# Attention values gathered by group of heads, a modulation slab moved ahead of a branch weight, and four filler matmuls taken out

## The chip, the cores and the metric

The kernel runs on one core of one Trainium2 chip. The metric is the device time of one execution in microseconds (us).

## The reference

Two transformer blocks are computed in sequence on 256 tokens of width 1024, in fp32. The part that the change touches lies in the first block's token mixer: eight attention heads of 64 values share two key and value heads, and the mixer's two branches are then merged.

```python
def blocked_bidirectional_gqa(q, k, v):
    ...
        s = jnp.einsum('bhgqd,bhkd->bhgqk', qblk, kt) * scale
        p = jax.nn.softmax(s, axis=-1)
        return jnp.einsum('bhgqk,bhkd->bhgqd', p, vt)
...
    ya = jnp.einsum('bsw,wd->bsd', o_att.astype(h.dtype), w_branch_att)
    yh = jnp.einsum('bsw,wd->bsd', o_hg.astype(h.dtype), w_branch_hg)
    g = jax.nn.sigmoid(gate_logits.astype(f32)).reshape(B, S, N_BRANCHES, D)
    merged = (g[:, :, 0] * ya.astype(f32) + g[:, :, 1] * yh.astype(f32)).astype(h.dtype)
    return jnp.einsum('bsd,de->bse', merged, w_out)
...
        x = x + gate1 * token_mixer(...)
        h = rms_norm(x, norm_ffn_w[l]) * (1.0 + scale2) + shift2
        x = x + gate2 * expert_choice_ffn(h, w_router[l], w_exp_gate[l], w_exp_up[l], w_exp_down[l])
```

`gate1`, `scale2` and so on are six vectors of 1024 values, products of the conditioning vector with `ada_w`. The mixer is followed by 16 experts (400 MB of weights) and by the second block.

## The kernel before, in words

Each engine has its own program, written out in order; semaphores tie them together. Three orders matter here.

**The weights.** SP loads slabs of 2 MB, in the order of `FIRST_SLABS`, into a ring of three slots (`slot_of`), then the experts' slabs. `slab_free` makes SP wait until the slot's slab before has been used. A slab of `ada_w` (`ada4`, `ada5`, ...) is read by TensorE as it lies. All others (`W9`, `W10`, `att`, `hg`, `out0`, ...) are first split by half slab, called a chunk: ScalarE writes a rounded part (line 784), VectorE the remainder (line 1287), and TensorE multiplies three times (lines 2069 to 2071). There are three chunk buffers. `att` is the weight of the attention branch; its halves are the chunks of the jobs `ya0` and `ya1`. `hg` and `yh0`, `yh1` are the same for the other branch.

**PSUM.** Work on TensorE is cut into jobs. The list `JOBS` gives each job one of four pairs of PSUM banks, and `begin` makes a job wait until the job before it on its pair is drained.

**The tail of the mixer on TensorE** is, in order: `a_values` for two halves of heads of token tile 0 (jobs `pv00`, `pv01`, line 2243), `W9`, the same for tile 1 (`pv10`, `pv11`), `ada9`, a transpose, `ada4`, the small column job `adc9`, the first half of `W10`, the row job `adr4`, the second half of `W10`, `ada5`, `ya0`, `adr5`, `ya1`, `yh0`, `yh1`. An `ada` job (line 2156) multiplies a slab by the conditioning vector; VectorE copies the result out (`ada_part`, line 1339); the row job (line 2177) sums it and repeats it over all partitions, and VectorE adds it to the bias (`ada_row`, line 1356). `adr4` and `adr5` make the two halves of `gate1`, which is first read after `mo0`.

In `a_values`, `b` picks two of the four heads of a group and their output goes to PSUM partitions 64b to 64b+63, 256 columns wide. `attended` (line 1523) copies it to `oattT`, whose four blocks of 128 rows so follow the natural order of the 512 rows of `w_branch_att`.

Earlier, `level(0)` issues four matmuls on constant data (`spin_into`, line 2080), whose result is overwritten, before it waits for its inputs (`factors_ready` and the draining of `W0`).

Of the kernel before, what the change touches and what calls it, by code (L numbers as in the profile page):

```python
# [14 lines left out]
P = 128  # L15
S = 256
T = S // P
D = 1024
# [43 lines left out]

# [15 lines left out]
FIRST_SLABS = (  # L78
    [(f"ada{i}", f"ada{i}") for i in range(4)]
    + [(n, n) for n in ("W1", "W2", "W0", "W4", "W5", "W3", "W6", "W7", "ada6", "W8", "ada7")]  # L80
    + [(n, n) for n in ("W9", "ada8", "ada9", "W10", "ada4")] + [("att", "ya1"), ("ada5", "ada5"), ("hg", "yh1")]
    + [("out0", "mo0"), ("ada10", "ada10"), ("ada11", "ada11"), ("out1", "mo1")]
)
A_SLABS = [("v0", "v0"), ("v1", "v1"), ("u0", "u0"), ("u1", "u1"), ("am0", "am0"), ("am1", "am1")]
# [102 lines left out]
ARRIVED, BEFORE, _count, _last = [], [], [0] * (R + 4), [None] * (R + 4)  # L187
for _n in range(AT_FFN[1] + 2 * FJ):
    _s = slot_of(_n)
    _count[_s] += 16  # L190
    ARRIVED.append(_count[_s])
    BEFORE.append(_last[_s])
    _last[_s] = _n
# [11 lines left out]
def build(nc, A, out):  # L205
    with ExitStack() as ctx:
# [339 lines left out]
        def _(sp):  # L546
# [34 lines left out]
            for name, _ in FIRST_SLABS:  # L581
                n = SLAB_AT[name]
                if name.startswith("ada"):
                    load(n, columns(A["ada_w"][0], int(name[3:]) * NB))
                elif name == "W5":
                    load(n, columns(A["w_in"][0], W_COLS[name], 256), dst=kn(n)[:, :, 0:256])
                elif name.startswith("W"):
                    load(n, columns(A["w_in"][0], W_COLS[name]))
                elif name in ("att", "hg"):
                    load(n, A[f"w_branch_{name}"][0].rearrange("(k p) n -> p k n", p=P), 4)  # L590
                else:
                    load(n, columns(A["w_out"][0], int(name[3:]) * NB))

# [676 lines left out]
        def _(dve):  # L1270
# [247 lines left out]

            def attended(job, t, g):
                wait_full(dve, job)  # L1520
                dst = oattT.rearrange("p (i s) -> p i s", i=4)[:, 2 * g:2 * g + 2, t * P:(t + 1) * P]
                src = bank(job, 0)[:, 0:S].rearrange("p (i s) -> p i s", i=2)
                dve.tensor_copy(dst, src).then_inc(psum_drained[pair(job)], 1)

            maxima(0, "sc00")
# [44 lines left out]
            ada_part(4)  # L1570
            ada_col(9)
            split_to(CHUNK_OF["ya0"])
            dve.wait_ge(bias1_in, 32)
            ada_row(4, gate1[:, 0:NB])
            split_to(CHUNK_OF["ya1"])
            ada_part(5)
            split_to(CHUNK_OF["yh0"])

            for job in ("W7", "W8"):
# [1 line left out]
            for n in range(2):  # L1581
                job = f"ya{n}"
                wait_full(dve, job)
                for t in range(T):
                    dve.tensor_tensor(merged[:, t, n * NB:(n + 1) * NB], bank(job, t),
                                      gsig[:, 0, t, n * NB:(n + 1) * NB], ALU.mult).then_inc(psum_drained[pair(job)], 1)

                if n == 0:
                    ada_row(5, gate1[:, NB:D])
                split_to(CHUNK_OF["yh1"] + n)  # L1590
            for job in ("W9", "W10"):
                wait_drained(dve, job)
# [443 lines left out]
        def _(pe):  # L2036
# [163 lines left out]
            def level(lv):  # L2200

                job = f"lv{lv}"
                begin(job)
                if lv == 0:
                    spin_into(4, bank(job, 1)[:, 0:S])
                if lv:
                    pe.wait_ge(exp_ready, 4 * lv - 2)
                pe.wait_ge(factors_ready, lv + 1)
                queries = EQ[lv % 2] if lv else gq
                if lv == 0:  # L2210
                    wait_drained(pe, "W0")
                for t in range(T):
                    for h in range(HG):
                        qry = t if lv < LEVELS - 1 else 1 - t
                        ins = mm(bank(job, t)[:, h * P:(h + 1) * P], EK[lv % 2][:, h, t * P:(t + 1) * P],
                                 queries[:, h, qry * P:(qry + 1) * P], start=True, stop=True)
                end(ins, job)
# [17 lines left out]
            def a_values(t, g):  # L2235
# [2 lines left out]
                wait_drained(pe, f"PT{t}{g}")  # L2238
                begin(job)
                for k in range(2):  # L2240
                    heads = ptr[g][:, k * NB:(k + 1) * NB].rearrange("p (j b s) -> p b j s", j=2, b=2)
                    for b in range(2):
                        ins = mm(PS[64 * b:64 * b + 64, 2 * pair(job), 0:S], va[:, k, 64 * g:64 * g + 64], heads[:, b],
                                 start=k == 0, stop=k == 1)
                end(ins, job)

            def gated_values():
# [52 lines left out]
            turn("ohgT", [ohg[:, t, i * P:(i + 1) * P] for i in range(4) for t in range(T)])  # L2300
            ada_part(4)
            ada_col(9)
            natural("W10", hT, lambda: ada_row(4))
            ada_part(5)
            pe.wait_ge(oatt_low, 1)
            branch("ya0", oattR)
            ada_row(5)
            branch("ya1", oattR)
            wait_drained(pe, "ohgT")
            for n in range(2):  # L2310
                branch(f"yh{n}", ohgR)
# [443 lines left out]
```

## Time and profile before

| | |
|---|---|
| median of 3 runs | 1819.2 us (1819.18 to 1823.26) |
| the profiled execution: its own time | 1823.26 us |
| the profiled execution: span from first to last instruction | 1821.4 us |
| mean granted TensorE clock | 0.888 |
| busy: TensorE, VectorE, ScalarE, GpSimd | 81%, 32%, 26%, 5% of the span |
| busy in the chain that ended last | DMA 45%, TensorE 42%, VectorE 6% |

The profile has a page with shares of the span, and views that can be asked of any stretch: the instructions in order of time (a timeline), busy time by stretch, and the chain of work that ended last. In a timeline a row is start, duration, engine, line, operation, what is written and read, count of merged instructions, and in brackets the idle time before it with what ended it. One fp32 matmul appears as two records. In a row by stretch, the columns are: stretch, its length, then busy time (and instructions) of TensorE, its weight loads, VectorE, ScalarE and GpSimd, then the granted clock as a share of 2.4 GHz, the busy share of the DMA engines, and GB/s. The mixer fills the first 285 us or so, the experts follow until about 1200 us, then the second block.

### The profile page before, as it was taken

The page shows a single profiled execution, that of the slowest core. Times are in us where ns is not written, and L with a number is a line of the kernel's source. Part 1 is how long each engine was busy: PE and PEld are TensorE (multiplying, and loading weights), DVE is VectorE, ACT ScalarE, POOL GpSimd, SP SyncE. Part 2 cuts the span into 40 slices and gives each one's busy share as a digit, 9 for nine tenths or more (in the row PEclk, how much of TensorE's full clock was granted, in tenths as well). Part 3 has the DMA queues.
Part 4 walks back from the last instruction along what each step waited for, and adds up shares of the span by engine and source line. Part 5 has one row for each costly group of instructions (what it writes and reads, how often), then busy time and mean ns, then how long its engine had stood idle before and what let it go on. Part 6 is the DMA issues. An engine that isn't in the chain of part 4 may idle for free.

```text
span 1821.4 us, 21033 instructions
## 1 busy us (share of the span) xinstructions
PE 1471.9 (81%) x8909; PEld 932.2 (51%) x8909; DVE 582.5 (32%) x749; ACT 467.0 (26%) x660; POOL 89.5 (5%) x77
## 2 busy tenths in 40 slices
PE   4999998777666776677667667679999989979998
PEld 1987674222221222123212222138799978869997
DVE  3488463000000000000000000037665555755553
ACT  3676322000000000000000000035554445664442
POOL 1591000000000000000000000000000000000000
PEclk8999998977888877887778877879999999999999
DMA  9536789999999999999999999994455535425540
GB/s 353 172 123 224 269 331 368 427 429 428 429 429 429 427 430 427 429 429 426 431 427 429 429 427 431 425 365 170 175 194 187 187 140 200 147 93 185 185 185 24
DMA packets 97860, 565.30 MB, mean 310 GB/s; under 512 B 4764, under 2 KB 6056, under 8 KB 73224
## 3 DMA queue, kind: packets, MB, share of 16 engines
q1 hardware_dynamic: 95064, 555.81, 75.3%
q0 software_dynamic: 2112, 7.06, 1.3%
q10 hardware_dynamic: 624, 1.57, 0.3%
q8 instruction: 46, 0.75, 0.2%
q14 instruction: 14, 0.11, 0.0%
HBM read 563.37 MB, written 1.05 MB: 310 GB/s over the span
## 4 chain that ended last, share of the span: by engine, by line
DMA 45%; PE 42%; DVE 6%; ACT 3%; issue 3%; POOL 1%; SPq 0%; DVEq 0%; ACTq 0%; POOLq 0%
DMA ring_b<-in_w_exp_up_dram 22%; DMA ring_b<-in_w_exp_down_dram 22%; PE PS L2069 10%; PE PS L2070 10%; PE PS L2071 10%; PE PS L2415 3%; PE PS L2439 2%; DVE parts L1287 2%; PE PS L2052 1%; DMA ring_a<-in_ada_w_dram 1%; PE PS L2156 1%; ACT parts L784 1%; DVE rounded L1287 1%; PE PS L2383 1%; ACT junk L802 1%
## 5 line engine op out<-in xcount | busy, mean ns | idle before, releaser
L1287 DVE TENSOR_TENSOR parts<-ring_a,parts 128x2048 fp32r<-128x2048 f32 (+1 forms) x101 | 234.6, 2326 | 151.5 <-ACT parts L784 150.9
L2415 PE MATMUL PS<-ring_a,arena 128*32 128x512 f32 x1232 | 180.5, 717 | 107.2 <-DMA ring_a<-in_w_exp_up_dram 63.5
L784 ACT ACTIVATE parts<-ring_a 128x2048 fp32r<-128x2048 f32 (+1 forms) x101 | 191.3, 1899 | 163.6 <-PE PS L2071 154.9
L2415 PE MATMUL PS<-ring_b,arena 128*32 128x512 f32 x768 | 127.5, 798 | 104.6 <-DMA ring_b<-in_w_exp_up_dram 66.5
L1720 DVE TENSOR_TENSOR arena<-PS,arena 128x512 f32<-128x512 f32 x16 | 11.1, 692 | 568.8 <-PE PS L2415 568.8
L2415 PEld LDWEIGHTS PS<-ring_a,arena 128*32 128x32 f32 x1232 | 36.3, 120 | 243.9 <-DMA ring_a<-in_w_exp_up_dram 104.2
L1023 ACT ACTIVATE arena<-PS 128x512 f32<-128x512 f32 x16 | 9.6, 597 | 564.1 <-PE PS L2415 564.1
L2069 PE MATMUL PS<-parts,hT 128*128 128x512 f32 (+1 forms) x352 | 131.0, 372 | 10.3 <-issue 3.4
L2069 PE MATMUL PS<-hT,parts 128*128 128x256 f32 x448 | 128.1, 286 | 8.0 <-POOL hT L670 8.0
L2439 PE MATMUL PS<-ring_b,arena 128*32 128x512 f32 x720 | 101.7, 699 | 39.6 <-DMA ring_b<-in_w_exp_down_dram 39.6
L2415 PEld LDWEIGHTS PS<-ring_b,arena 128*32 128x32 f32 x768 | 23.9, 128 | 204.6 <-DMA ring_b<-in_w_exp_up_dram 105.4
L2070 PE MATMUL PS<-hT,parts 128*128 128x256 f32 x448 | 127.7, 285 | 0.0
L2071 PE MATMUL PS<-hT,parts 128*128 128x256 f32 x448 | 127.7, 285 | 0.0
L2070 PE MATMUL PS<-parts,hT 128*128 128x512 f32 (+1 forms) x352 | 127.3, 362 | 0.0
L2071 PE MATMUL PS<-parts,hT 128*128 128x512 f32 (+1 forms) x352 | 127.2, 361 | 0.0
L2069 PE MATMUL PS<-parts,rounded 128*128 128x512 f32 x248 | 100.0, 403 | 3.6 <-DVE rounded L1908 1.8
L2071 PE MATMUL PS<-parts,rounded 128*128 128x512 f32 x248 | 99.0, 399 | 0.0
L2070 PE MATMUL PS<-parts,rounded 128*128 128x512 f32 x248 | 98.8, 399 | 0.0
L2383 PE MATMUL PS<-arena,xn 128*128 128x32 f32 x512 | 90.8, 350 | 0.5 <-DVE arena L1690 0.5
L2383 PEld LDWEIGHTS PS<-arena,xn 128*128 128x128 f32 x512 | 90.9, 276 | 0.6 <-DVE arena L1690 0.6
L2069 PEld LDWEIGHTS PS<-hT,parts 128*128 128x128 f32 x448 | 86.4, 193 | 9.0 <-POOL hT L670 8.1
L1030 ACT ACTIVATE arena<-PS 128x512 f32<-128x512 f32 x16 | 9.6, 597 | 311.8 <-PE PS L2426 311.8
(333 smaller groups left out, 2171.0 us busy)
## 6 DMA issues: line engine op xcount, KB each, us to landing
ring_a<-in_w_exp_gate_dram SPq DMA_DIRECT2D x45, 2048.0 KB, 25.5
ring_b<-in_w_exp_down_dram SPq DMA_DIRECT2D x45, 2048.0 KB, 26.1
ring_a<-in_w_exp_up_dram SPq DMA_DIRECT2D x32, 2048.0 KB, 25.7
ring_b<-in_w_exp_up_dram SPq DMA_DIRECT2D x32, 2048.0 KB, 26.5
ring_a<-in_w_exp_down_dram SPq DMA_DIRECT2D x16, 2048.0 KB, 27.1
ring_b<-in_w_exp_gate_dram SPq DMA_DIRECT2D x16, 2048.0 KB, 23.4
ring_a<-in_w_up_dram SPq DMA_DIRECT2D x16, 2048.0 KB, 7.8
ring_a<-in_w_down_dram SPq DMA_DIRECT2D x16, 2048.0 KB, 7.7
```

Source lines behind the costliest of these rows:

```text
L784: act.activation(part_of(c, 0), raw(c), ACT.Copy).then_inc(chunk_high, 1)
L802: act.activation(junk[:, NB:D], x_half(n, t, half), ACT.Square, accum_out=ssq[:, n, t, half:half + 1]).then_inc(norm_ssq, 1)
L1287: dve.tensor_tensor(part_of(c, 1), raw(c), part_of(c, 0).bitcast(F32), ALU.subtract)\
L1720: dve.tensor_tensor(hid, PS[:, 1, :], sg, ALU.mult).then_inc(hid_ready, 1)
L2052: ins = nc.tensor.transpose(bank(job, i // 4)[:, (i % 4) * P:(i % 4 + 1) * P], src, ident)
L2069: mm(out, left[0], right[0], start=start, stop=False)
L2070: mm(out, left[0], right[1], start=False, stop=False)
L2071: return mm(out, left[1], right[0], start=False, stop=stop)
L2156: ins = mm(PS[32 * j:32 * j + 32, 2 * pair(job), :], crep[:, 2 * j + i, :], kn(n)[:, 2 * j + i, :], start=i == 0, stop=i == 1)
L2383: ins = mm(PS[:, 1, k * CAP:(k + 1) * CAP], xn[:, t, paired(k)], onehot[:, t, :], start=t == 0, stop=t == 1)
L2415: ins = mm(PS[32 * j:32 * j + 32, side, :], xe[:, 2 * q + kk, :], w[:, kk, j * NB:(j + 1) * NB], start=q == 0 and kk == 0, stop=q == 3 and ...
L2439: ins = mm(PS[32 * q:32 * q + 32, 2 + n, :], hidT[:, q, 32 * i:32 * i + 32], w[:, q, n * NB:(n + 1) * NB], start=i == 0, stop=i == 3)
```

## The change

Four things are changed.

1. `a_values` makes, for each group `g` of four heads, two matmuls of 512 columns into PSUM partitions 64g to 64g+63, in place of four of 256 columns into both halves of the partitions. `attended` copies 64 partitions by 512 columns. Rows of `oattT` are now ordered by (group, value) in the partition and by head in the block.
2. The slab `att` has to follow that order. It is loaded by two transfers of 1 MB, one into partitions 0 to 63 and one into 64 to 127.
3. `ada5` is loaded before `att` instead of after it, its job runs between the halves of `W10` ahead of `adr4`, and `adr5` runs before `ya0`. VectorE's order follows.
4. The four matmuls at the head of `level(0)` are gone.

```diff
-    + [("ada4", 1, 3), ("adc9", 1, 0), ("W10", 2, 3), ("adr4", 1, 2), ("ada5", 1, 0)]
-    + [("ya0", 2, 1), ("adr5", 1, 2), ("ya1", 2, 0), ("yh0", 2, 2), ("yh1", 2, 3)]
+    + [("ada4", 1, 3), ("adc9", 1, 0), ("W10", 2, 3), ("ada5", 1, 0), ("adr4", 1, 2), ("adr5", 1, 0)]
+    + [("ya0", 2, 1), ("ya1", 2, 0), ("yh0", 2, 2), ("yh1", 2, 3)]
...
-    + [(n, n) for n in ("W9", "ada8", "ada9", "W10", "ada4")] + [("att", "ya1"), ("ada5", "ada5"), ("hg", "yh1")]
+    + [(n, n) for n in ("W9", "ada8", "ada9", "W10", "ada4", "ada5")] + [("att", "ya1"), ("hg", "yh1")]
...
-    _count[_s] += 16
+    _count[_s] += 32 if _n == SLAB_AT["att"] else 16
...
+                elif name == "att":
+
+                    for g in range(2):
+                        src = A["w_branch_att"][0, g * 256:(g + 1) * 256, :].rearrange("(i d) n -> d i n", d=AHD)
+                        load(n, src, dst=kn(n, 4)[64 * g:64 * g + 64])
...
             def attended(job, t, g):
                 wait_full(dve, job)
-                dst = oattT.rearrange("p (i s) -> p i s", i=4)[:, 2 * g:2 * g + 2, t * P:(t + 1) * P]
-                src = bank(job, 0)[:, 0:S].rearrange("p (i s) -> p i s", i=2)
+                dst = oattT.rearrange("p (i s) -> p i s", i=4)[64 * g:64 * g + 64, :, t * P:(t + 1) * P]
+                src = PS[64 * g:64 * g + 64, 2 * pair(job), :].rearrange("p (i s) -> p i s", i=4)
...
             split_to(CHUNK_OF["ya0"])
+            ada_part(5)
             dve.wait_ge(bias1_in, 32)
             ada_row(4, gate1[:, 0:NB])
             split_to(CHUNK_OF["ya1"])
-            ada_part(5)
+            ada_row(5, gate1[:, NB:D])
             split_to(CHUNK_OF["yh0"])
...
-                if n == 0:
-                    ada_row(5, gate1[:, NB:D])
...
                 job = f"lv{lv}"
                 begin(job)
-                if lv == 0:
-                    spin_into(4, bank(job, 1)[:, 0:S])
...
                 for k in range(2):
-                    heads = ptr[g][:, k * NB:(k + 1) * NB].rearrange("p (j b s) -> p b j s", j=2, b=2)
-                    for b in range(2):
-                        ins = mm(PS[64 * b:64 * b + 64, 2 * pair(job), 0:S], va[:, k, 64 * g:64 * g + 64], heads[:, b],
-                                 start=k == 0, stop=k == 1)
+                    ins = mm(PS[64 * g:64 * g + 64, 2 * pair(job), :], va[:, k, 64 * g:64 * g + 64],
+                             ptr[g][:, k * NB:(k + 1) * NB], start=k == 0, stop=k == 1)
...
-            natural("W10", hT, lambda: ada_row(4))
-            ada_part(5)
+            natural("W10", hT, lambda: (ada_part(5), ada_row(4)))
+            ada_row(5)
             pe.wait_ge(oatt_low, 1)
-            branch("ya0", oattR)
-            ada_row(5)
-            branch("ya1", oattR)
+            for n in range(2):
+                branch(f"ya{n}", oattR)
```

## Rows read from the trace of the kernel before

**Rows 1.** The page: busy TensorE, and the granted clock in 40 slices.
```profile
PE 1471.9 (81%) x8909; PEld 932.2 (51%) x8909; DVE 582.5 (32%) x749; ACT 467.0 (26%) x660; POOL 89.5 (5%) x77
...
PEclk8999998977888877887778877879999999999999
```

**Rows 2.** The chain that ended last, 0 to 330 us: start, us, what.
```profile
215.19 0.86 PE PS L2177 x2
...
327.12 26.29 DMA ring_b<-in_w_exp_up_dram
```

**Rows 3.** Timeline of SP's queue: att, ada5, then three expert loads.
```profile
205.74 0.37 SPq L571 DMA_DIRECT2D ring_a<-in_w_branch_att_dram  x1
206.15 0.51 SPq L571 DMA_DIRECT2D ring_a<-in_ada_w_dram  x1
...
246.08 2.73 SPq L571 DMA_DIRECT2D arena<-in_w_exp_gate_dram  x2
...
275.90 0.33 SPq L571 DMA_DIRECT2D ring_b<-in_w_exp_gate_dram  x1
...
305.24 2.22 SPq L571 DMA_DIRECT2D arena<-in_w_exp_down_dram  x2
```

**Rows 4.** Timeline of PE: before and at the first matmuls of level 0.
```profile
86.83 1.89 PE L2080 MATMUL PS<-crep 128*128 128x256 f32 x8
89.18 4.12 PE L2215 MATMUL PS<-arena 128*128 128x128 f32 x32 [0.46 <-ACT arena L921]
```

**Rows 5.** Busy time by stretch, 120 to 140 us.
```profile
120.00:130.00 10.00, 9.40 (x56) 8.16 (x55) 9.90 (x7) 9.94 (x12) 10.00 (x6) 1.00 0.07 24
130.00:140.00 10.00, 7.54 (x40) 6.05 (x39) 9.90 (x13) 6.72 (x9) 6.40 (x5) 1.00 0.59 210
```

**Rows 6.** Timeline of PE: pv00 and pv01, then adc7; the score matmuls of 161 us.
```profile
182.96 1.08 PE L2243 MATMUL PS<-tmp,arena 128*64 128x256 f32 x8
...
184.83 1.10 PE L2166 MATMUL PS<-mean,junk 128*128 128x1 f32 x8
...
161.03 4.91 PE L2225 MATMUL PS<-arena 64*128 64x256 f32 x32
```

**Rows 7.** Timeline of ACT: the splits of att and of hg.
```profile
213.60 3.72 ACT L784 ACTIVATE parts<-ring_a 128x2048 fp32r<-128x2048 f32 x2 [4.80 <-DMA ring_a<-in_w_branch_att_dram]
...
224.14 1.92 ACT L784 ACTIVATE parts<-ring_a 128x2048 fp32r<-128x2048 f32 x1 [1.49 <-DMA ring_a<-in_w_branch_hg_dram]
```

**Rows 8.** ada5's load of 206.15: us from issue to landing.
```profile
DMA to landing us min/median/max: 12.8/12.8/12.8
```

**Rows 9.** Timeline of PE: W10's first matmul, adr4, ya0's first matmul.
```profile
209.45 0.48 PE L2069 MATMUL PS<-parts,hT 128*128 128x512 f32 x1
...
215.02 1.03 PE L2177 MATMUL PS<-arena,mean 128*128 128x512 f32 x2
...
223.32 0.50 PE L2069 MATMUL PS<-parts,rounded 128*128 128x512 f32 x1
```

**Rows 10.** Timeline of DVE: attended, split of ya0, ada_row(4), ada_part(5).
```profile
184.09 0.42 DVE L1523 COPY arena<-PS 128x256 f32<-128x256 f32 x1 [1.47 <-PE PS L2243]
...
215.55 2.29 DVE L1287 TENSOR_TENSOR parts<-ring_a,parts 128x2048 fp32r<-128x2048 f32 x1 [5.76 <-ACT parts L784]
217.76 0.68 DVE L1356 TENSOR_TENSOR arena<-arena,PS 128x512 f32<-128x512 f32 x1
...
223.45 0.69 DVE L1339 COPY arena<-PS 128x512 f32<-128x512 f32 x1 [2.81 <-PE PS L2156]
```

**Rows 11.** Busy time by stretch, 265 to 270 us, the highest rate there.
```profile
265.00:270.00 5.00, 5.00 (x23) 4.12 (x22) 2.40 (x4) 0.72 (x2) 0.00 (x0) 1.00 1.02 433
```

**Rows 12.** An idle TensorE and what followed: by stretch, and PE's first row after it.
```profile
39.00:42.00 3.00, 0.00 (x0) 0.00 (x0) 2.94 (x5) 3.00 (x4) 1.95 (x2) 0.52 1.05 386
...
48.00:50.00 2.00, 2.00 (x13) 2.00 (x13) 2.00 (x1) 0.00 (x0) 0.00 (x0) 0.66 0.95 26
...
44.64 0.58 PE L2069 MATMUL PS<-hT,parts 128*128 128x256 f32 x1 [8.01 <-POOL hT L670]
```

More of the change, by code:

```diff
@@ L588, in _ @@
                     load(n, columns(A["w_in"][0], W_COLS[name]))
-                elif name in ("att", "hg"):
-                    load(n, A[f"w_branch_{name}"][0].rearrange("(k p) n -> p k n", p=P), 4)
+                elif name == "att":
+                    for g in range(2):
+                        src = A["w_branch_att"][0, g * 256:(g + 1) * 256, :].rearrange("(i d) n -> d i n", d=AHD)
+                        load(n, src, dst=kn(n, 4)[64 * g:64 * g + 64])
+                elif name == "hg":
+                    load(n, A["w_branch_hg"][0].rearrange("(k p) n -> p k n", p=P), 4)
                 else:
```

## The prediction

> **What bounds the kernel now.** I read the page first. TensorE is busy for four fifths of the span, and its granted clock is nearly full at both ends of it and lower in the middle [rows 1]: the middle is the experts, where TensorE waits for weights. Then I read the chain that ended last. Once the first slabs are in, it runs through the compute engines up to 327 us; from there on its long pieces are expert weights arriving [rows 2]. So the kernel is a mixer bound by compute, then a stream of weights that can't go faster, then a second block. The question is whether a delay in the mixer is given back by the stream. SP's queue answers it: the stream's early loads are each issued when TensorE or a split has freed a slot, at 246, 275.9 and 305.2 us [rows 3]. A mixer that ends d later issues all of them d later, with the same bytes behind them. I count each microsecond on TensorE's path between 160 and 285 us in full.
>
> **Part 4, the four matmuls.** They take 86.83 to 88.7 us, after which TensorE still waits 0.46 us for ScalarE's W0 results [rows 4]. Without them TensorE waits from 86.83 to 89.18, and level 0 starts at the same moment: 0 us. What covers this is ScalarE's work before line 921. The other bound is the clock. A gap of 2.35 us in a stream that was granted full clock may cost a stretch at 1.2 GHz; half speed over the next 3.4 us would lose 1.7 us. Behind it lie waits that can take this up: in 120 to 140 us TensorE is idle for 0.6 + 2.46 = 3.06 us, while VectorE is busy for 19.8 of 20 us [rows 5]. That stretch is VectorE's, and TensorE arrives early. I take 0, bounds 0 and +1.7.
>
> **Part 1, the values.** Today two jobs take 184.83 - 182.96 = 1.87 us [rows 6]: 16 records in 8 pairs, two column halves side by side, 0.23 us a pair. The new job is two fp32 matmuls of 512 columns into the same 64 columns of the array, so inside a job nothing runs side by side. One such matmul costs 0.86 us [rows 2]. Two jobs are four of them: 3.44 us if nothing overlaps, 1.72 us if the jobs overlap fully, since they use opposite halves. The nearest row is the score matmuls, where consecutive jobs also use opposite halves (of the rows): 32 records in 4.91 us [rows 6]. At 0.23 us that would be 7.4 us in sequence and 3.7 us fully side by side; if each job overlaps only half of the next (20 steps) it is 4.6 us, nearest to the 4.91. I take half an overlap: 0.75 x 3.44 = 2.58 us, or +0.7 us for each of the two pairs of jobs. Sum +1.4 us, bounds -0.3 and +3.1. The Trainium skill (TensorEngine Tiling (Array Packing), Key Properties) says that tiles operate independently and can load and multiply in parallel; by that alone the overlap would be full and this term -0.3 us. The score row shows only part of it.
>
> VectorE's copy goes from 0.42 us (256 columns) to about 0.69 us (512 columns) [rows 10], four times. The values are read only after oattT's split, and that was finished by about 208 us, 15 us before ya0; the copies hide behind W9 and W10.
>
> **Part 3, the order.** TensorE does the same jobs in another order, so without waits it is 0 us. Waits decide. Times from here are those of the trace before; part 1 shifts them all alike.
>
> ada5 now takes the place of att in the queue. It is issued when ada9 is done, at 205.7, and lands where att landed, at 213.6 [rows 7]. TensorE wants it when W10's first half ends, at 215.0 [rows 9]: no wait, with 1.4 us to spare.
>
> att comes second. Before, the second slab (ada5) landed at 206.15 + 12.8 = 218.95 [rows 3, 8], and the third (hg) at 224.1 [rows 7]: 5.3 us for each 2 MB.
>
> What is late next? adr5 now stands ahead of ya0 and needs ada5 copied out by VectorE. VectorE does that behind the split of ya0, which waits for att. From the landing: ScalarE's first chunk, then VectorE's start, 215.55 - 213.60 = 1.95 us; the split until the next instruction, 217.76 - 215.55 = 2.21 us; the copy, 0.69 us [rows 7, 10]. So ada5 is drained 4.85 us after att lands. TensorE is ready for adr5 at 223.3, where ya0 begins today [rows 9]. If att lands at 218.95, adr5 can start at 223.8: a wait of 0.5 us. Behind adr5 the chunk of ya0 is ready, and the attention operand long since. So every microsecond by which att is later than 218.5 is a microsecond of TensorE's path.
>
> **Part 2, the two half-wide transfers.** The trace before has no large transfer to 64 partitions. Lower bound: both halves together take what one slab takes, 5.3 us. Upper bound: the highest rate in the neighbourhood is 433 GB/s into 128 partitions [rows 11], or 3.4 GB/s for each. For att to keep up, each partition would have to take twice what any row shows while its half is being written. At 3.4 GB/s a partition each half takes as long as a whole slab: 10.6 us, and att lands at 213.6 + 10.6 = 224.2. I take the upper end, as the rows reach only that rate for a partition. It means ada5 drained at 229.05 and a wait of 5.7 us ahead of adr5, where the kernel before has none. The second chunk is split about 4 us later, well before ya1 needs it; hg lands at 229.5 and its chunk at about 235, before yh0 at 241. So nothing adds to the 5.7.
>
> The Trainium skill (SBUF — State Buffer, "Door 1: The DMA port swizzle") states that 64 partitions reach 8 of 16 ports: 196 GB/s against 328 for 128 partitions, at 1 MiB. Its section "Can I just issue two DMAs to hit both halves?" says that two such transfers serialize. As an estimate from that page, att takes 2 x 5.35 = 10.7 us and the wait is 5.8 us. No row here tests it.
>
> **The clock after the wait.** TensorE was idle for 8.0 us up to 44.64; the granted clock had fallen (0.52 in 39 to 42 us), and it was back at full only at about 49.4 us (0.66 over 48 to 50 us) [rows 12]. So 4.7 us of matmuls ran at 1.2 GHz and 2.4 us were lost. After 5.7 us of idling I expect much of that: +2.0 us, bounds 0 and +2.4. The work that it slows is ya0, on the path.
>
> **Sum.** 0 + 1.4 + 5.7 + 2.0 = +9.1 us. The durations come from the profiled execution, which took 1823.26 us, 4 us above the median, with its span of 1821.4 us. Over its own time the sum gives 1832.4 us; the median of the runs is 1819.2, and I put the difference on that: 1828.3 us. A difference under 0.3% (5.5 us) is about what a measurement of this kernel can't tell from none.
>
> **The rivals.**
>
> *Not slower: the half-wide transfers keep the full rate* (part 2 at its lower bound). The 16 DMA engines may spread over both transfers, as both are in the queue together. Then 0 + 1.4 + 0.5 + 0 = +1.9 us, 1821.1 us. It decides above some 300 GB/s for att: 2.1 MB then take 7 us, and the wait is 2.2 us. For it: DMA queues here show no width at which they fall off. Against it: the rate for a partition would be new.
>
> *The clock at level 0 is not hidden*: the gap at 86.83 us costs 1.7 us and VectorE's levels wait for it, on top of the forecast: 1830.0 us. For it: TensorE was fully busy from 100 to 120 us. Against: the 3.06 us of waits in [rows 5].
>
> *The move does nothing and the values gain*: full overlap (-0.3), att early enough (0.5), 1819.4 us. Nothing in the trace gives a gain of over 5.5 us; only a clock better placed in the later stages could, and I see no reason for that.
>
> **How the numbers follow.** Half rate for att, level 0 hidden: 0.60. Half rate and level 0 not hidden: 0.07. Full rate, +1.9 us: 0.23. Full rate with full overlap: 0.06. Something else that gains: 0.04. The time is that of the first, 1828.3 us; its own range is from -0.3 + 5.7 + 0 = +5.4 to 3.1 + 5.7 + 2.4 = +11.2 us, 1824.6 to 1830.4 us. With the second case (to 1832) and down to the middle of the third, the range is 1820.5 to 1831.5 us. Slower by over 0.3%: the two half-rate cases less a small part near +5.4 us, 0.63. Within 0.3%: 0.33. Faster: 0.04.
>
> **What would show it.** In the profile after: two issues for att, and ScalarE's split of ya0 starting about 18.5 us after ada5's issue (right) or 13 us (wrong); the DMA rate near 215 GB/s at a busy share of 1 while att moves; VectorE's copy of ada5 behind the split of ya0, and TensorE waiting 5 to 6 us for it ahead of line 2177; the granted clock below 1 after that; two value jobs in about 2.6 us; level 0 starting no later than before against its neighbours; and the loads of the experts later by the same sum. The prediction is wrong if att's two halves move together at full rate, or if the stream of experts gives the delay back.

## The result and the profile after

The kernel after the change takes 1831.99 us (median of 6 runs, 1830.21 to 1837.72), the kernel before in the same comparison 1823.01 us (6 runs, 1819.18 to 1824.18). The ratio is 1.0058 with a 95% interval of 1.0042 to 1.0074: slower, by about 10.6 us of 1823 (7.7 to 13.5 by the interval), or 9.0 us between the medians. All 31 executions of after on record lie between 1826.29 and 1839.0 us, with a median of 1833.1. The forecast was 1828.3 us, +9.1 us on a base of 1819.2. The forecast difference lies inside the interval; the time lies 0.5 us above the range.

The profiled execution took 1833.11 us, with a span of 1831.2 us and a mean granted clock of 0.881 (before: 0.888). The page, busy engines and the granted clock in 40 slices [rows 1]:

```profile
PE 1481.5 (81%) x8885; PEld 932.3 (51%) x8885; DVE 583.4 (32%) x749; ACT 466.6 (25%) x660; POOL 89.4 (5%) x77
...
PEclk8999998977887788877777877779999999999999
```

TensorE has 24 records fewer and is busy 9.6 us longer: nearly the same work at a lower clock. Only 1.5 us of the 9.6 lie between W1 and the end of the mixer; 7.8 us lie among the experts, where TensorE waits for weights and the stretch is no longer than before. The timeline of SP's queue shows the new order, ada5 (the second of the two issues merged in the first row, at 209.7) and then two issues for att [rows 3]:

```profile
192.73 17.37 SPq L571 DMA_DIRECT2D ring_a<-in_ada_w_dram  x2
210.14 1.75 SPq L571 DMA_DIRECT2D ring_a<-in_w_branch_att_dram  x2
212.61 0.38 SPq L571 DMA_DIRECT2D ring_a<-in_w_branch_hg_dram  x1
...
258.48 2.73 SPq L571 DMA_DIRECT2D arena<-in_w_exp_gate_dram  x2
...
288.29 0.33 SPq L571 DMA_DIRECT2D ring_b<-in_w_exp_gate_dram  x1
...
316.90 2.08 SPq L571 DMA_DIRECT2D arena<-in_w_exp_down_dram  x2
```

The three expert loads are issued at 258.5, 288.3 and 316.9 us, 12.4, 12.4 and 11.7 us later than in [rows 3], 2.9 us of it from a stretch ahead of everything changed (first row of the table below). The time from issue to landing, for ada5 and then for the two halves of att [rows 8]:

```profile
DMA to landing us min/median/max: 8.9/8.9/8.9
...
DMA to landing us min/median/max: 13.3/15.3/17.3
```

ada5 lands at 218.6 us, the halves of att at 223.5 and 228.5 us. The busy time by stretch shows why. While att moves, the DMA engines are fully busy and bring half of what they bring for the slabs around it:

```profile
213.00:215.00 2.00, 2.00 (x11) 1.73 (x12) 0.64 (x2) 0.00 (x0) 0.00 (x0) 1.00 1.05 408
219.00:221.00 2.00, 2.00 (x18) 0.42 (x16) 0.00 (x0) 0.00 (x0) 0.00 (x0) 1.00 1.04 211
223.00:225.00 2.00, 2.00 (x10) 1.65 (x9) 0.00 (x0) 0.00 (x0) 0.00 (x0) 1.00 1.02 207
229.00:231.00 2.00, 0.00 (x0) 0.00 (x0) 0.50 (x1) 2.00 (x2) 0.00 (x0) 1.00 1.01 401
231.00:235.00 4.00, 1.46 (x3) 0.84 (x3) 4.00 (x4) 3.80 (x4) 0.00 (x0) 0.55 1.04 395
235.00:238.00 3.00, 3.00 (x8) 2.04 (x7) 3.00 (x3) 0.35 (x1) 0.00 (x0) 0.50 1.06 371
238.00:240.00 2.00, 2.00 (x10) 1.63 (x9) 0.99 (x1) 0.00 (x0) 0.00 (x0) 0.94 1.00 356
```

The last three rows are the granted clock behind the wait: 0.55, 0.50, and nearly full from 238 on. The chain of work that ended last, between 211 and 235 us, names each link of that wait:

```profile
211.19 17.34 DMA ring_a<-in_w_branch_att_dram
228.53 0.02 issue
228.56 1.92 ACT parts L789
230.47 0.02 issue
230.50 0.04 DVE parts L1292
230.53 2.17 issue
232.71 0.69 DVE arena L1344
233.40 0.14 issue
233.54 2.04 PE PS L2181 x2
```

It is read from the top: att's second half, ScalarE's first chunk, VectorE's split of it, and only then the copy of ada5, whose input had been in PSUM since 221 us. TensorE's timeline shows the price [rows 6, 9]: the value jobs of token tile 0, the first and last of 8 records and what follows; ada5's job and adr4; the last matmul of W10; adr5.

```profile
186.52 0.64 PE L2243 MATMUL PS<-tmp,arena 128*64 128x512 f32 x1
186.53 0.64 PE L2243 MATMUL PS<-arena 128*64 128x512 f32 x1
...
187.87 0.59 PE L2243 MATMUL PS<-arena 128*64 128x512 f32 x1
188.39 1.10 PE L2170 MATMUL PS<-mean,junk 128*128 128x1 f32 x8
190.15 1.92 PE L2160 MATMUL PS<-ring_a,crep 128*32 128x512 f32 x16 [0.65 <-DVE modc L1354]
...
219.21 1.92 PE L2160 MATMUL PS<-ring_a,crep 128*32 128x512 f32 x16
221.07 1.13 PE L2181 MATMUL PS<-arena,mean 128*128 128x512 f32 x2
...
227.29 0.39 PE L2075 MATMUL PS<-parts,hT 128*128 128x512 f32 x1
233.54 2.04 PE L2181 MATMUL PS<-arena,mean 128*128 128x512 f32 x2 [5.86 <-DVE arena L1344]
```

Lined up by the same jobs on TensorE (start, before and after), the difference of the two profiled executions splits up:

| from ... to | before, us | after, us | difference |
|---|---|---|---|
| start to W1, the first weight job | 44.64 | 47.50 | +2.9 |
| to level 0 | 44.54 | 43.80 | -0.7 |
| to the last level (level 8) | 59.12 | 60.57 | +1.45 |
| to ada8 | 37.89 | 38.28 | +0.4 |
| to ada9 | 17.56 | 17.60 | 0 |
| to the transpose behind mixer (mTa) | 43.36 | 51.77 | +8.4 |
| to the last expert's down matmuls | 960.9 | 960.0 | -0.9 |
| to the end | 613.35 | 611.65 | -1.7 |

The sum is +9.8 us, the difference of the spans. The first row lies ahead of everything changed: in the profiled executions of this study W1 starts between 43.0 and 49.1 us, whatever the kernel. From W1 to mTa, where all four changes lie, before takes 202.5 us and after 212.0 us: +9.5 us, made of -0.7 + 1.45 + 0.4 + 8.4. The stream of experts gives back less than 1 us: from mTa to the last expert every profiled execution took 957.5 to 960.9 us (960.9 in before), and the time doesn't depend on when mTa comes (958.7 us both with mTa at 244.9 us, in e11, and at 260.7 us, in e5).

### The profile page after: what moved, and what is told of

It reads as the page before. It is cut to its first block, busy times and chain, and to the rows that moved or that the text cites. A ratio compares the mean times of both kernels' runs of the same rounds, so it can differ in the third digit from the quotient of the medians.

```text
span 1831.2 us, 21000 instructions
## 1 busy us (share of the span) xinstructions
PE 1481.5 (81%) x8885; PEld 932.3 (51%) x8885; DVE 583.4 (32%) x749; ACT 466.6 (25%) x660; POOL 89.4 (5%) x77
## 4 chain that ended last, share of the span: by engine, by line
DMA 45%; PE 41%; DVE 6%; ACT 3%; issue 3%; POOL 1%; SPq 0%; DVEq 0%; ACTq 0%; POOLq 0%
DMA ring_b<-in_w_exp_down_dram 20%; DMA ring_b<-in_w_exp_up_dram 20%; PE PS L2073 10%; PE PS L2075 10%; PE PS L2074 10%; PE PS L2414 3%; PE PS L2438 2%; DVE parts L1292 2%; DMA ring_a<-in_a_w_in_dram 2%; DMA ring_a<-in_w_exp_up_dram 1%; PE PS L2056 1%; PE PS L2160 1%; DMA ring_a<-in_w_branch_att_dram 1%; ACT parts L789 1%; DMA arena<-in_ada_w_dram 1%
## 5 line engine op out<-in xcount | busy, mean ns | idle before, releaser
L2414 PE MATMUL PS<-ring_b,arena 128*32 128x512 f32 x768 | 130.9, 817 | 105.3 <-DMA ring_b<-in_w_exp_up_dram 64.9
L2438 PE MATMUL PS<-ring_b,arena 128*32 128x512 f32 x720 | 103.9, 712 | 39.0 <-DMA ring_b<-in_w_exp_down_dram 39.0
```

Source lines behind the costliest of these rows:

```text
L2414: ins = mm(PS[32 * j:32 * j + 32, side, :], xe[:, 2 * q + kk, :], w[:, kk, j * NB:(j + 1) * NB], start=q == 0 and kk == 0, stop=q == 3 and ...
L2438: ins = mm(PS[32 * q:32 * q + 32, 2 + n, :], hidT[:, q, 32 * i:32 * i + 32], w[:, q, n * NB:(n + 1) * NB], start=i == 0, stop=i == 3)
```

## The experiments

Three theories about the main term were put against each other. *Ports*: the half-wide transfers move at half rate because partitions 0 to 63, or 64 to 127, reach only half of the ways into SBUF, as the prediction cites from the Trainium skill (SBUF — State Buffer, "Door 1: The DMA port swizzle"). *Per partition*: each partition takes no more than 3.4 GB/s, which was the prediction's reason. *Order*: the wait comes from the new order, whatever the width. Beside them stood the smaller terms, the fillers and the values. Each group below was timed against the kernel before on the same chip.

**The parts one by one.** For these four, the kernel before took 1820.76 us (median of 35 runs).

*Without the four matmuls (part 4 alone).*

```diff
                 begin(job)
-                if lv == 0:
-                    spin_into(4, bank(job, 1)[:, 0:S])
```

> The kernel before without the four matmuls at the head of level 0, nothing else. The prediction's term: 0 us, level 0 starts on time and what the clock takes is hidden. Rival, from the trace after the change (clock 0.53 in 91.4 to 95 us, later levels shifted by about 1.3 us and never caught up): +1.3 us, ratio about 1.0007, and in the trace a low granted clock right behind level 0's start and ScalarE waiting over 1 us for level 0's matmuls.

1820.55 us, ratio 1.0004 (0.9993 to 1.0014). In TensorE's and ScalarE's timelines, and by stretch:

```profile
88.55 5.44 PE L2213 MATMUL PS<-arena 128*128 128x128 f32 x32 [2.18 <-ACT arena L921]
```
```profile
91.42 2.36 ACT L895 ACTIVATE arena<-arena 128x512 f32<-128x512 f32 x4 [0.77 <-PE PS L2213]
```
```profile
89.60:93.00 3.40, 3.40 (x18) 3.40 (x17) 3.22 (x4) 2.63 (x4) 0.82 (x1) 0.51 0.03 7
```

The gap of 2.18 us does lower the clock: the row of 32 records, the matmuls of levels 0 and 1, takes 5.44 us where it took 4.12 [rows 4], and the granted clock is 0.51 for 3.4 us. ScalarE's work on the level's result waits for them, so it is not hidden: level 0 to the last level takes 59.82 us where it took 59.12, +0.7 us. Level 2 starts 1.3 us late against level 0; 0.6 us of that is made up between levels 5 and 6. That is too small for the timing to show.

*The order alone (part 3), att in one transfer.*

```diff
-    + [("ada4", 1, 3), ("adc9", 1, 0), ("W10", 2, 3), ("adr4", 1, 2), ("ada5", 1, 0)]
-    + [("ya0", 2, 1), ("adr5", 1, 2), ("ya1", 2, 0), ("yh0", 2, 2), ("yh1", 2, 3)]
+    + [("ada4", 1, 3), ("adc9", 1, 0), ("W10", 2, 3), ("ada5", 1, 0), ("adr4", 1, 2), ("adr5", 1, 0)]
+    + [("ya0", 2, 1), ("ya1", 2, 0), ("yh0", 2, 2), ("yh1", 2, 3)]
...
-    + [(n, n) for n in ("W9", "ada8", "ada9", "W10", "ada4")] + [("att", "ya1"), ("ada5", "ada5"), ("hg", "yh1")]
+    + [(n, n) for n in ("W9", "ada8", "ada9", "W10", "ada4", "ada5")] + [("att", "ya1"), ("hg", "yh1")]
...
```

> The kernel before with part 3 alone (ada5 loaded and multiplied ahead, adr5 before ya0); att comes in one transfer to 128 partitions. The prediction: att lands 5.3 us after ada5, TensorE waits 0.5 us ahead of adr5, the time stays within 0.1% of before. Rival, that the order itself costs (VectorE copies ada5 only behind a split that waits for att, whatever the transfer's width): a wait of 5 us or more ahead of adr5 and +6 to +9 us.

1821.52 us, ratio 1.0005 (0.9993 to 1.0017). TensorE's row of adr5:

```profile
223.46 1.10 PE L2176 MATMUL PS<-arena,mean 128*128 128x512 f32 x2 [0.19 <-DVE arena L1339]
```

A wait of 0.19 us, and ada9 to mTa takes 43.79 us instead of 43.36. The order costs next to nothing as long as att comes at full rate. The theory of the order alone falls.

*The two half-wide transfers alone (part 2), in the old order and with the old rows.*

```diff
...
+                elif name == "att":
+                    for p0, p1 in ((0, 64), (64, 128)):
+                        src = A["w_branch_att"][0].rearrange("(k p) n -> p k n", p=P)[p0:p1]
+                        load(n, src, dst=kn(n, 4)[p0:p1])
...
```

> The kernel before with part 2 alone: att in two transfers of 64 partitions each, the same rows as before, in the old place ahead of ada5. At half rate att lands 10.6 us after its transfer starts in place of 5.3, so ada5 lands at about 224.2 on the scale of before and TensorE, ready at 221.5, waits 2.7 us for it; ya0's split is ready by 223.1 and costs nothing more: +2.8 us, up to +4 with the clock. Rival, full rate for both halves together: no wait, 0 us. Rival, the place in the queue doesn't matter: a wait of 5.9 us here as well.

1826.48 us, ratio 1.0029 (1.0017 to 1.0042): +5.3 us by the ratio. The landing of the halves, and the row of ada5's job, which has the slower att ahead of it in the queue:

```profile
DMA to landing us min/median/max: 8.1/10.2/12.2
```
```profile
228.26 3.23 PE L2160 MATMUL PS<-ring_a,crep 128*32 128x512 f32 x16 [2.71 <-DMA ring_a<-in_ada_w_dram]
```

TensorE waits 2.71 us, and ada5's job takes 3.23 us instead of 1.9: the clock again. ada9 to mTa takes 47.45 us, +4.1; the timing shows somewhat more than the trace. So the width of the transfers costs time in either order, and more in the new one.

*The kernel after with att in one transfer* (the attention output then meets the weight's rows in another pairing).

```diff
...
-                    for g in range(2):
-                        src = A["w_branch_att"][0, g * 256:(g + 1) * 256, :].rearrange("(i d) n -> d i n", d=AHD)
-                        load(n, src, dst=kn(n, 4)[64 * g:64 * g + 64])
+                    load(n, A["w_branch_att"][0].rearrange("(k p) n -> p k n", p=P), 4)
```

> The changed kernel with att in one transfer to 128 partitions, in the old row order (so the attention branch multiplies rows in another order than its values; the work is the same). The prediction's cause, the half-wide transfers: the wait ahead of adr5 falls from 5.9 to about 0.5 us, the low clock behind it goes, and 8 of the 9 us come back, leaving +1.5 to +2.5 us over before. Rival, that order or fillers are the cause: still +6 us or more.

1824.79 us, ratio 1.0009 (0.9995 to 1.0022): by the ratio about 0.5% of the 0.58% is gone. By the medians 4.0 us over before are left, and in the trace W1 to mTa is still 2.1 us longer than before. TensorE's row of adr5:

```profile
226.61 1.10 PE L2179 MATMUL PS<-arena,mean 128*128 128x512 f32 x2 [0.90 <-DVE arena L1342]
```

The wait falls from 5.86 to 0.90 us and ada9 to mTa from 51.77 to 44.59 us. This is the main result: most of the loss is the half-wide transfers, through the wait for ada5's copy.

**Why the transfers are slow, and what stands behind them.** For these four, the kernel before took 1820.26 us (median of 9 runs).

*att in four transfers of 32 partitions.* By the port theory, partitions 0 to 31 are as good as 0 to 63; by a limit for each partition, the rate would halve again, to about 109 GB/s.

```diff
...
-                    for g in range(2):
+                    for p0, p1 in ((0, 32), (32, 64), (64, 96), (96, 128)):
+                        g = p0 // 64
                         src = A["w_branch_att"][0, g * 256:(g + 1) * 256, :].rearrange("(i d) n -> d i n", d=AHD)
-                        load(n, src, dst=kn(n, 4)[64 * g:64 * g + 64])
+                        load(n, src[p0 % 64:p0 % 64 + p1 - p0], dst=kn(n, 4)[p0:p1])
```

> The changed kernel with att in four transfers of 32 partitions each (0-31, 32-63, 64-95, 96-127), same rows and places. The measured rate while the half-wide transfers move is 211 to 227 GB/s; what sets it? Theory A, the one my prediction argued with, is a limit of 3.4 GB/s for each partition: 32 partitions then take 109 GB/s, att takes about 19 us and lands 9 us later than with halves. Theory B, the Trainium skill's ports (SBUF — State Buffer, Door 1: 0..31 reach the same 8 ports as 0..63): still about 215 GB/s, 10 us in all, landing as with halves and a wait of about 6 us ahead of adr5.

1833.9 us, span 1832.0. This kernel and the next two were executed once each, so that the rates and waits in their traces count here and not their times. The rate by stretch while att moves, then TensorE's row of adr5:

```profile
219.00:221.00 2.00, 2.00 (x12) 1.30 (x15) 0.00 (x0) 0.00 (x0) 0.00 (x0) 1.00 1.03 211
223.00:225.00 2.00, 2.00 (x9) 1.38 (x8) 0.00 (x0) 0.00 (x0) 0.00 (x0) 1.00 1.02 227
227.00:229.00 2.00, 2.00 (x10) 1.50 (x8) 0.00 (x0) 0.00 (x0) 0.00 (x0) 1.00 1.00 221
```
```profile
234.49 2.04 PE L2183 MATMUL PS<-arena,mean 128*128 128x512 f32 x2 [5.29 <-DVE arena L1346]
```

211 to 227 GB/s, with half the partitions. Each partition now takes 6.6 to 7.1 GB/s, twice what the prediction called a limit. That reason falls. The Trainium skill (SBUF — State Buffer, "Door 1: The DMA port swizzle") says that a partition 32 further on lies on the same port and one 64 further on lies on the cluster's other port, so that partitions 0 to 31 and 0 to 63 reach the same 8 ports; the trace agrees, with 211 to 227 GB/s here beside 207 to 227 for the halves in after.

*Transfers of partitions 0 to 31, 32 to 95 and 96 to 127* (the weight's rows in the old order). The middle one has 64 partitions like att's halves, but straddles the middle.

```diff
...
-                    for g in range(2):
-                        src = A["w_branch_att"][0, g * 256:(g + 1) * 256, :].rearrange("(i d) n -> d i n", d=AHD)
-                        load(n, src, dst=kn(n, 4)[64 * g:64 * g + 64])
+                    for p0, p1 in ((0, 32), (32, 96), (96, 128)):
+                        src = A["w_branch_att"][0].rearrange("(k p) n -> p k n", p=P)[p0:p1]
+                        load(n, src, dst=kn(n, 4)[p0:p1])
```

> The changed kernel with att in three transfers: partitions 0-31, 32-95, 96-127 (rows in the old order, so the attention branch pairs rows and values differently; same work). Theory A (3.4 GB/s for each partition): 4.8 us each, 14.4 us in all. Theory B (ports by the number's bits; 32..95 reaches 8 + 8 ports): the middle 1 MB moves at about 430 GB/s in 2.4 us, the outer halves of a MB at 215 in 2.4 us each, 7.3 us in all against 10 with halves, and the wait ahead of adr5 falls from about 6 to about 3.5 us. A third view, that only the width of one transfer counts: the middle one no faster than 215 GB/s, 10 us in all.

1828.31 us, span 1826.3. By stretch, one row while each of the three moves:

```profile
215.00:217.00 2.00, 2.00 (x17) 0.92 (x19) 0.00 (x0) 0.00 (x0) 0.00 (x0) 1.00 1.01 201
217.00:219.00 2.00, 2.00 (x13) 0.69 (x5) 0.00 (x0) 0.00 (x0) 0.00 (x0) 1.00 1.00 391
219.00:221.00 2.00, 2.00 (x10) 1.65 (x9) 0.00 (x0) 0.00 (x0) 0.00 (x0) 1.00 1.07 225
```

This is the cleanest reading of the study: 64 partitions in one transfer of 1 MB, 391 GB/s. Between 32 and 64 partitions, not the count decides but whether they lie in one half or in both. The rows have the plain order of e3, whose halves were slow, so the order of the rows isn't the cause either. The wait ahead of adr5 is 3.65 us.

*The four quarters in mixed order: 0 to 31, 64 to 95, 32 to 63, 96 to 127.* If transfers that follow one another overlapped, neighbours in opposite halves would fill both sets of ports.

```diff
...
-                    for g in range(2):
+                    for p0, p1 in ((0, 32), (64, 96), (32, 64), (96, 128)):
+                        g = p0 // 64
                         src = A["w_branch_att"][0, g * 256:(g + 1) * 256, :].rearrange("(i d) n -> d i n", d=AHD)
-                        load(n, src, dst=kn(n, 4)[64 * g:64 * g + 64])
+                        load(n, src[p0 % 64:p0 % 64 + p1 - p0], dst=kn(n, 4)[p0:p1])
```

> As the four quarters, but in the order 0-31, 64-95, 32-63, 96-127, so that neighbours in the queue are on opposite halves. If neighbours in one queue can move side by side, att lands up to 4.7 us earlier than with halves (rate up to 430 GB/s). If they are served one behind the other, as the landing times of the two halves in the trace after suggest (5 us apart), the rate stays near 215 GB/s; between the two, small transfers that overlap at their edges: 9 us in place of 10.

1833.43 us, span 1831.4; 229, 215, 236 and 238 GB/s in four stretches of 2 us, and a wait of 4.51 us. They gain little on the 207 to 227 GB/s of after, far from the full rate, as if the transfers passed nearly one behind the other. The Trainium skill (SBUF — State Buffer, "Can I just issue two DMAs to hit both halves?") says that two transfers at once, one into each half, serialize and gain only a few per cent; these rates agree.

*The kernel after with VectorE's copy of ada5 ahead of the split of ya0.* It takes the copy out of the wait for att.

```diff
-            split_to(CHUNK_OF["ya0"])
             ada_part(5)
+            split_to(CHUNK_OF["ya0"])
```

> The changed kernel, but VectorE copies ada5 out before it splits ya0's chunk. My step: adr5 waits for VectorE's copy, which stands behind the split, so the late att blocks adr5 too. Then here adr5 runs without a wait inside the gap, and ya0 waits for its own chunk: landing + 4.15 us. The gap becomes about 4.2 us in place of 5.9 (0.7 us of copy and 0.9 us of adr5 leave the path), 1.5 to 2.5 us faster than the changed kernel (which was 1.0058 of before), so about 1.0045. Rival, that the wait was for something else than the split: nothing changes.

1828.73 us (median of 5 runs, 1826.08 to 1831.06), ratio 1.0038 (1.0025 to 1.0052), against 1.0058 (1.0042 to 1.0074) for after. The intervals overlap, and the medians show almost nothing, so that the gain is shown by the trace alone. VectorE's copy, and TensorE's adr5 and first matmul of ya0:

```profile
217.98 0.69 DVE L1344 COPY arena<-PS 128x512 f32<-128x512 f32 x1 [7.43 <-PE PS L2160]
```
```profile
224.30 1.02 PE L2181 MATMUL PS<-arena,mean 128*128 128x512 f32 x2
...
229.22 0.47 PE L2073 MATMUL PS<-parts,rounded 128*128 128x512 f32 x1 [3.89 <-DVE parts L1292]
```

adr5 no longer waits, but ya0 behind it waits 3.89 us for att's first chunk. So two thirds of the wait are att's late arrival itself, and one third is where the copy stands in VectorE's order (3.89 of 5.86 us are left). ada9 to mTa takes 49.15 us, +5.8 instead of +8.4.

**The small terms, and the clock early on.** For these four, the kernel before took 1821.6 us (median of 31 runs, 1819.18 to 1827.4).

*The kernel after with the four matmuls put back.*

```diff
                 begin(job)
+                if lv == 0:
+                    spin_into(4, bank(job, 1)[:, 0:S])
```

> The changed kernel with the four matmuls put back at the head of level 0. From the traces: no low clock behind level 0, 0.5 to 1.4 us back, the wait ahead of adr5 unchanged at 5.9 us with its 2.5 us of slow clock. So about 1.0050 of before (the changed kernel was 1.0058). Rival, that the fillers carry most of the loss: 1.002 or less.

1828.93 us (8 runs, 1826.38 to 1834.29), ratio 1.0040 (1.0024 to 1.0055), against 1.0058 (1.0042 to 1.0074) for after; the intervals overlap. In the trace level 0 to the last level takes 59.12 us again. From W1 to the last level it is 103.5 us, 0.9 us less than after, and the wait ahead of adr5 is 5.19 us.

*The values alone (part 1)*, with the weight's rows left as they were.

```diff
...
-                    heads = ptr[g][:, k * NB:(k + 1) * NB].rearrange("p (j b s) -> p b j s", j=2, b=2)
-                    for b in range(2):
-                        ins = mm(PS[64 * b:64 * b + 64, 2 * pair(job), 0:S], va[:, k, 64 * g:64 * g + 64], heads[:, b],
-                                 start=k == 0, stop=k == 1)
+                    ins = mm(PS[64 * g:64 * g + 64, 2 * pair(job), :], va[:, k, 64 * g:64 * g + 64],
+                             ptr[g][:, k * NB:(k + 1) * NB], start=k == 0, stop=k == 1)
```

> The kernel before with part 1 alone, the new matmuls and copies of the attention values; the branch weight keeps its old row order, so the branch pairs rows and values differently, same work. My term was +1.4 us. From the trace after: the two jobs of a pair start 10 ns apart and take 1.87 us as before, and only ada8 waits 0.4 us longer behind VectorE's longer copies: +0.4 us, within 0.1% of before. Rival, half overlap: 2.6 us for a pair of jobs and +1.4 us.

1821.58 us (10 runs), ratio 0.9993 (0.9981 to 1.0006). The last two records of the pair of jobs, then adc7 and ada8:

```profile
189.09 0.59 PE L2241 MATMUL PS<-tmp,arena 128*64 128x512 f32 x1
189.10 0.59 PE L2241 MATMUL PS<-arena 128*64 128x512 f32 x1
189.62 1.10 PE L2166 MATMUL PS<-mean,junk 128*128 128x1 f32 x8
191.37 1.07 PE L2156 MATMUL PS<-ring_a,crep 128*32 128x512 f32 x8 [0.65 <-DVE modc L1349]
```

The pair begins at 187.75 us: 1.87 us up to adc7, as in [rows 6]. The jobs overlap in full. What part 1 costs is the 0.65 us that ada8 waits for VectorE, behind the longer copies: +0.4 us on TensorE's path.

*The kernel before with fillers in the gap ahead of W1*, to see whether the clock at 40 to 50 us [rows 12] can be kept up.

```diff
+            spin_into(14, PS[:, 5, 0:S])
             pe.wait_ge(low_out, 2)
```

> Built on the kernel before: 14 matmuls on constant data, result unused, in the 8 us in which TensorE waits ahead of W1 (36.6 to 44.6 us in the trace before, with W1's first 4.7 us at half the clock). If the clock is what such a wait costs, the granted clock stays at 1 over 39 to 50 us and 2.4 us come back: ratio 0.9987. Rival, that the mixer's other chains set the pace there: the clock rises and the time stays.

1821.51 us (12 runs), ratio 0.9998 (0.9987 to 1.0008). The fillers end 1.9 us before W1. W1 now starts at 42.96 us at the full clock, but less than 1 us later the clock falls all the same:

```profile
44.00:46.00 2.00, 2.00 (x11) 2.00 (x11) 2.00 (x2) 0.69 (x1) 2.00 (x4) 0.50 1.05 386
```

*The same, with 6 more ahead of ada0, 3 ahead of ada1 and 3 ahead of ada2's job.*

```diff
+            spin_into(6, PS[:, 5, 0:S])
             ada_part(0)
+            spin_into(3, PS[:, 5, 0:S])
             ada_part(1)
...
+            spin_into(3, PS[:, 5, 0:S])
             ada_part(2)
```

> As the one before, with 6 more such matmuls ahead of ada0 and 3 each ahead of ada1 and ada2, in waits for slabs. In profiled runs W1 starts between 44.1 and 49.1 us, by how long the clock stays low between 21 and 42 us. If these fillers keep it up, W1 starts at 44 us each time, the runs spread less, and the median gains another 1 us: ratio 0.998 of before. Rival: they delay ada0 and nothing is gained over 14 alone.

1818.61 us (12 runs, 1816.12 to 1822.88), ratio 0.9979 (0.9968 to 0.9990): the fastest kernel of the study, some 3 to 4 us below before. How it gains isn't settled. In its one profiled execution (1822.76 us, the second slowest of the twelve) the granted clock was still low from 20.6 to 30.8 us, and W1 began at 47.43 us, no earlier than elsewhere.

## Why the prediction came out as it did

- **The half rate of att was right, the reason for it wrong.** Forecast: near 215 GB/s; measured: 207 to 227, so the first rival, full rate, is out. But "each partition would have to take twice what any row shows" is not a limit: quarters took that twice (e5), and 64 partitions across the middle moved at 391 GB/s (e6). The estimate from the Trainium skill (SBUF — State Buffer, "Door 1: The DMA port swizzle"), set beside the sum, had the mechanism that fits both.
- **The wait ahead of adr5**: forecast 5.7 us, measured 5.86. ScalarE's split of ya0 began 18.8 us after ada5's issue; 18.5 was forecast. The chain of its links was read as it turned out, and e8 shows both parts of it.
- **The clock behind it**: forecast +2.0. Over ada9 to mTa, 8.41 - 5.86 = 2.55 us are left beside the wait. Of these 0.2 to 0.3 us belong to the new order, put at 0 in the prediction: e2 and e4, with no low clock there, are 0.24 and 0.33 us longer beside their waits. The clock's share is so about 2.3 us, inside the bounds.
- **The values**: forecast +1.4, measured +0.4. "I take half an overlap" was wrong: jobs in opposite halves of the columns overlap fully, unlike the score jobs in opposite halves of the rows. The copies, called hidden, are what costs.
- **The fillers**: forecast 0, measured +0.7 us. Level 0 to the last level takes 1.45 us longer in after, but the stretch ahead of it is 0.7 us shorter. From W1 to the last level after takes 104.4 us and before 103.7. In all seven profiled executions without the four matmuls it is 104.2 to 104.4 us. With them it is 103.5 to 103.7 in before, e2, e3 and e9; e11 and e12, with more fillers ahead of W1, have 103.1, and e10, where the clock stayed low for longer behind W1's start, 104.3. "Behind it lie waits that can take this up" was right only in part. Level 2 came 1.3 us late in six of the seven; in e1, e4, e6 and e8 0.6 to 1.0 us of that was made up by level 7, in after and e5 nothing. The mechanism was the second rival's; the size lay between 0 and its 1.7. The 3.4 us that the prediction put at half speed stand in none of its rows; e1's row of 0.51 shows a stretch of that length.
- **The stream gives nothing back**: right, to within 1 us of 960 between before and after, and within 3.4 us over all profiled executions.
- **The sum.** 5.86 + 2.55 + 0.4 + 0.7 = 9.5 us from W1 to mTa, against 9.1. That the sum is so close is luck in part: the values came out 1.0 us below their term, and the fillers, the clock, the order and the wait together 1.4 us above theirs.
- **The base, the step that failed**: "the median of the runs is 1819.2, and I put the difference on that". Of its three runs, two lay at the bottom of a spread and one 4 us higher. The kernel before had its median at 1823.0 in the comparison with after (6 runs, the three among them), and at 1820.8 (35 runs), 1820.3 (9) and 1821.6 (31) in the others; over all 81 it is 1821.3, 2.1 us above the base. The measured time lies 3.7 us above the forecast: 2.1 us for the base, 0.4 us for the terms, and 1.2 us that no term accounts for and that is small beside the spread of the executions. On 1821.3 the same +9.1 gives 1830.4, inside the range but still 1.6 us short. That 1823.0 + 9.1 = 1832.1 meets the measured 1831.99 is luck: that median of 6 is high among the four, and the ratio gives 10.6 us. The forecast as a ratio, 1828.3 / 1819.2 = 1.0050, lies in the measured interval. The range had taken in every unknown cost of the change and nothing for the base.

What stays open: why before's executions differ by 4 to 8 us. They differ in the profile in where W1 starts (43.0 to 49.1 us), after stretches at low clock of different length. In before, e1, e2, e10 and e11, whose times the runs don't tell apart, the spans of the profiled executions differ by 6.9 us and the parts from W1 on by 3.0 us, so more than half of the spread arises ahead of W1; no run here separates the low clock as its cause. Also open is how e12 gains.

## What to carry to other kernels

With 32 partitions or more, it was which of them a load writes that decided its rate, and not how many: one half alone was slow, both halves in one transfer were fast. Before splitting a slab by partition to fit an operand's order, look for an order that one transfer to all partitions can bring. A late load costs not only what waits for it but all that its engine has queued behind it, here a copy whose input had been ready for over 11 us; the order on a serial engine should follow the arrival of inputs, and the idle time is paid a second time in the clock. A forecast of a time needs an allowance for its base: with three runs 4 us apart, the difference can be right within its interval and the time still miss.

## What the hardware showed that was not expected

- Partitions 32 to 95 took 391 GB/s; 0 to 31, 0 to 63 and 64 to 127 each 201 to 227 GB/s (up to 238 with quarters in mixed order), all at a DMA busy share of about 1. The DMA share doesn't tell a slow transfer from a fast one; the GB/s beside it does.
- Two fp32 jobs in opposite column halves, each 512 columns and two products, took 1.87 us together; one after the other they would be 3.44 us by adr4's 0.86 us a matmul [rows 2]. The score jobs, in opposite row halves, took 4.91 us [rows 6], between the prediction's 3.7 side by side and 7.4 in sequence.
- With TensorE idle for 2.2 us ahead of level 0, six of seven profiled executions had a stretch at 1.2 GHz behind it (granted 0.51 in e1, levels 0 and 1 in 5.44 us). With four small matmuls in the gap, none of seven had one (4.10 to 4.12 us). After 5.9 us of idling the clock stayed at or near 0.50 for another 4.7 us of work.
